# GLA stage of a FoX/GLA decoder step: weight tiles loaded two projection quarters sooner, the low part split one quarter later

## The reference, cut to what matters

```python
h = rmsnorm(x, ln_g)
z = h @ w_in                       # q, k, v, gates of both branches, merge gates
o_fox = softmax(q k^T * scale + forget sums) v      # prompt: causal; sample: over paged cache_k, cache_v
o_gla = scan over chunks of 64: att = tril((q e^b)(k e^-b)^T); o = att v + (q e^b) S; S = e^b_last S + ...
a = (o_fox * silu(fg)) @ w_up_a
b = (rmsnorm(o_gla) * silu(gg)) @ w_up_b
y = x + (sigmoid(ma) * a + sigmoid(mb) * b) @ w_out
```

## Time and profile before

| | us |
|---|---|
| median of 3 runs | 1595.02 (1590.80 to 1600.67) |
| the profiled execution | 1588.89 |
| its span, first to last instruction | 1587.2 |
| TensorE busy | 1447.4 (91%) |
| VectorE busy | 726.3 (46%) |
| ScalarE busy | 565.3 (36%) |
| GpSimd busy | 528.7 (33%) |
| mean granted TensorE clock, share of full | 0.972 |

### The profile page before, as it was taken

How to read it: one execution, slowest core, us unless ns; L and a number is a source line. 1 busy time by engine, 2 the same in 40 slices (tenths; PEclk the granted TensorE clock), 3 DMA queues, 4 the chain that set the end, 5 groups by cost and what they waited for, 6 DMA issues and landing times. The chain is left out here.

```text
span 1587.2 us, 43486 instructions
## 1 busy us (share of the span) xinstructions
PE 1447.4 (91%) x16281; PEld 1226.6 (77%) x16281; DVE 726.3 (46%) x1578; ACT 565.3 (36%) x1311; POOL 528.7 (33%) x953
## 2 busy tenths in 40 slices
PE   5999898989978897999989999889998899999998
PEld 5878777777767876788877888768876798888876
DVE  4344353543636555655546545655554223333221
ACT  6343444444532334323443334423334353111100
POOL 4444434440047135344353534454251122111000
PEclk9989999999989999999999999989999999999999
DMA  5131301222238688899997999879985764321521
GB/s 173 32 85 34 85 24 54 72 58 68 55 114 212 189 233 216 225 238 235 239 248 206 263 244 243 219 217 244 231 198 158 224 249 139 108 101 62 167 92 60
DMA packets 153411, 250.51 MB, mean 158 GB/s; under 512 B 45897, under 2 KB 58826, under 8 KB 152690
## 3 DMA queue, kind: packets, MB, share of 16 engines
q1 hardware_dynamic: 121618, 215.68, 49.8%
q0 software_dynamic: 31584, 32.04, 7.3%
HBM read 217.37 MB, written 30.22 MB: 156 GB/s over the span
## 5 line engine op out<-in xcount | busy, mean ns | idle before, releaser
L289 PE MATMUL psum<-h_hi,w_hi 128*128 128x384 f32 (+1 forms) x1344 | 491.0, 365 | 13.8 <-DVE q_fm L915 3.5
L289 PE MATMUL psum<-h_hi,w_lo 128*128 128x384 f32 (+1 forms) x1344 | 446.9, 332 | 0.0
L289 PE MATMUL psum<-h_lo,w_hi 128*128 128x384 f32 (+1 forms) x1344 | 446.4, 332 | 0.0
L1457 POOL DMA_DIRECT2D sc<-tmp_bias x512 | 278.3, 549 | 256.7 <-PE psum L1943 252.6
L289 PEld LDWEIGHTS psum<-h_hi,w_hi 128*128 128x128 f32 x1344 | 258.3, 192 | 67.1 <-issue 48.0
L289 PEld LDWEIGHTS psum<-h_lo,w_hi 128*128 128x128 f32 x1344 | 259.4, 193 | 2.7 <-issue 0.5
L289 PEld LDWEIGHTS psum<-h_hi,w_lo 128*128 128x128 f32 x1344 | 257.9, 192 | 0.0
L678 POOL DMA_DIRECT2D lfp<-in_cache_logf x256 | 124.1, 485 | 176.1 <-issue 176.1
L1671 DVE STREAM_TRANSPOSE k_page<-k_page 128x1024 f32<-128x1024 f32 x128 | 156.1, 1232 | 28.8 <-DMA k_page<-in_cache_k 27.8
L264 DVE TENSOR_TENSOR w_lo<-w_raw,w_hi 128x1024 fp32r<-128x1024 f32 x63 | 76.8, 1219 | 110.6 <-ACT w_hi L259 110.5
L259 ACT ACTIVATE w_hi<-w_raw 128x1024 fp32r<-128x1024 f32 x63 | 66.1, 1049 | 69.3 <-DMA w_raw<-in_w_tiles 37.9
(11 more groups left out here) (259 smaller groups left out, 2142.4 us busy)
## 6 DMA issues: line engine op xcount, KB each, us to landing
k_page<-in_cache_k SPq DMA_DIRECT2D x256, 256.0 KB, 3.8
v_page<-in_cache_v SPq DMA_DIRECT2D x256, 256.0 KB, 4.9
w_raw<-in_w_tiles SPq DMA_DIRECT2D x63, 512.0 KB, 5.6
g_pair<-tmp_gates SPq DMA_DIRECT2D x16, 544.0 KB, 4.6
sc<-tmp_bias POOLq DMA_DIRECT2D x512, 16.0 KB, 4.4
tmp_ogla<-gate POOLq DMA_DIRECT2D x4, 1088.0 KB, 6.8
g_pair<-tmp_ogla SPq DMA_DIRECT2D x8, 544.0 KB, 7.3
x_in<-in_x_prompt SPq DMA_DIRECT2D x8, 512.0 KB, 6.1
```

The costliest lines, as they stand in the source:

```text
L289: m = pe.matmul(out, wt[:, s, k, :], h[:, k, t0:t0 + w], start=(k == 0 and a == 0), stop=(k == KT_ - 1 and a == 2))
L1457: pool.dma_start(dst, src.unsqueeze(0).to_broadcast([TS, 2, 256])).then_inc(sc_in[j % SLOTS], 16)
```

## The change

Two conditions in `build_gla` are changed, nothing else. SP's `stream.load` moves from quarter (c = 1, part = 1) to quarter (c = 0, part = 3) of the same tile, past the steps that stand between these two in the list. VectorE's `split_lo` moves from quarter (0, 1) to quarter (0, 2). ScalarE's `split_hi` stays at (0, 1). No instruction is added or removed.

```diff
@@ build_gla, sync
             def z(n, c, part):
-                if c == 1 and part == 1:
+                if c == 0 and part == 3:
                     stream.load(sp, n)
@@ build_gla, vector
             def z(n, c, part):
-                if c == 0 and part == 1:
+                if c == 0 and part == 2:
                     stream.split_lo(dve, n)
```

## The result

The changed kernel takes 1588.05 us (median of 10 runs), the kernel before 1595.84 us in the same comparison; the ratio is 0.9948 with a 95% interval of 0.9923 to 0.9974. By that ratio it is 8.3 us less (0.52% of 1595.84), between 4 and 12; the medians lie 7.8 us apart. The profiled execution has a span of 1577.8 us against 1587.2; among the ten runs it is the fastest (1579.49 us), so the two profiles differ by a little more than the kernels do.

A forecast was written before the change was run, and what follows sets the result against it. TensorE was taken to bound the kernel, 741.1 of the stage's 810 us; 9.0 us from the low part plus 3 for the clock made 12.0, two thirds kept, 8 off 1595.0: 1587 us, range 1572 to 1604.

The forecast's parts named there:

- The total: Whole kernel: 8 us off the median of 1595.0, giving 1587 us; the GLA stage 6 to 10 us shorter.
- The low part: VectorE's split_lo, one quarter later, shortens TensorE's waits at n = 3, 6, 7, 23, 31, 32: 9.0 us.
- give-back: TensorE loses part of its gain at its next wait; two thirds of 12.0 us kept, 8 us.
- the clock: Half-clock stretches of TensorE after the waits at n = 31 and n = 7 go: 1.5 us each, 3 together.
- n = 31: TensorE's 2.38 us wait for the mask goes; the low part delays the next state by some 0.7; net 1.7 us.
- n = 7: TensorE's 3.43 us wait: transposition and gate step move into VectorE's waiting time, saving half, 1.7 us.
- n = 3: TensorE's 0.87 us wait: the low part's 1.2 us goes from ahead of the score step, saving 0.9 us.
- The load: SP's tile load sooner: ScalarE's tile waits fall from 35.9 to about 20 us; worth 0 to TensorE, bounds 0 and 16.
- its rival: More arrives: ScalarE's 16 us reach TensorE too, through the copies it makes in order; 1567 us, chance 0.08.
- SP at the low part: SP waiting for the low part before loading, at n = 1, 7, 24, 32: cost 0, without cover 11 us.
- Key pages: Loads ahead of key pages may delay VectorE's transposition: taken at 0, between a gain of 2 and a loss of 18 us.
- The rival built on it: Slower: 8 loads ahead of key pages delay VectorE and TensorE, 30 us less the 8 gained; 1617 us, chance 0.07.

The follow-up runs named there:

- Experiments 1 and 3: Against the kernel before, VectorE's low part one quarter later, load unmoved: in all tiles 0.9941; only at n = 3, 6, 7, 23, 31, 32 0.9937; only at the others 0.9969.
- experiment 2: Against the kernel before, the load alone two quarters sooner, low part unmoved: 1596.96 us, ratio 1.0019.
- experiment 5: Against the changed kernel, the load later, at quarter (2, 1), low part still at (0, 2): ratio to the kernel before 1.0149.
- experiment 8: Against the kernel before, the load two quarters sooner only at 8 tiles where it then precedes key pages: 0.9979; only at the 26 others: 1.0027.

## Why the prediction was right, point by point

*The total.* Forecast: 8 us off the median, 1587.0. Measured: 8.3 us (4 to 12), 1588.05. The stage was to be 6 to 10 us shorter and is 9.1 in the profiles. That the profiles come so close is in part luck: the 28 other tiles differ by 0.6 us only because TensorE stands 4.6 us longer in them while its matmuls take 4.1 us less, and nothing ties either to the low part.

*The low part.* This was the term that carried the sum, 9.0 us before give-back and 3 for the clock, kept at 8. Experiments 1 and 3 show it: alone it gives the whole, and at six tiles alone as well. Split as the forecast split it, the six tiles stand 6.9 us less where 9.0 were forecast, and have 2.7 us less in their matmuls where 3 were given to the clock. The clock's share fell at n = 31, as said, and at n = 23 and 32, which were not named; at n = 7 it went the other way. The waits of the earlier trace rows at n = 32, 31, 6 and 23 are gone but for 0.50 us at n = 32, and the next state of n = 31 is 0.73 us late, where 0.7 was forecast. By tile, forecast against the table above (with the clock stretch where one was named): n = 6 1.2 and 1.4; n = 23 1.3 and 1.9; n = 7 3.2 and 1.2; n = 31 3.2 and 3.0; n = 32 2.2 and 3.3; n = 3 0.9 and -1.2. The six sum to 12.0 and 9.6. At n = 7 the wait was there still, and half clock after it too, but the transposes come 1.8 us sooner, where 1.7 was forecast: that term was right and the clock's wrong.

n = 3 is where the forecast failed. The wait of 0.87 us went, and the next one took it. The score matmuls need ScalarE's last copy of the turned queries, which ends 14.9 us after the tile's start in both kernels; before and changed:

```profile
538.52 1.94 PE L1924 MATMUL psum<-k_page,q_row 128*32 128x64 f32 x64 [3.22 <-issue]
```

```profile
533.50 1.09 ACT L1506 ACTIVATE q_row<-psum 32x128 f32<-32x128 f32 x4
...
534.69 1.94 PE L1924 MATMUL psum<-k_page,q_row 128*32 128x64 f32 x64 [4.28 <-issue]
```

The profile names nothing for these two waits; that they end with the copy is read from the times (538.42 and 534.59). Behind the longer stand the clock stayed at half for longer: the projection matmuls that follow are granted 0.50 over 3.4 us in the changed kernel, and 0.72 over 2.4 us before. So a gain of 0.9 became a loss of 1.2. The tile has 20.8 to 22.7 us in the five profiles with its low part unmoved and 22.0 to 24.2 in the eight with it moved.

*The load.* Taken at 0 between -2 and +18; the load alone measured 1.0019, so +3 us with an interval of -2 to +8. The value taken stands. Of ScalarE's eight waits the first and the one at n = 18 stayed, 7.6 and 4.6 us, as argued. The third that was to stay (4.4 us, n = 28) and the 2.2 us that were to be left at n = 20 were ended by TensorE and no longer by the tile: `split_hi` also waits for the tile before to be projected, and that became the later of the two. So this wait fell to 12.2 us and not to 20, but ScalarE still stands at these two places, 3.54 and 5.59 us. Both kinds of its wait before the copy together fell from 56.5 to 44.0 us. The claim behind it, that these waits don't reach TensorE, is what experiment 2 shows, and experiment 5 that it ends. The rule that the forecast quoted from the Trainium skill (DMA: Bandwidth & Descriptors, Rules for kernel authors), to issue early and wait late, was borne out in part for ScalarE's waits (35.9 to 12.4 us with the load alone, two of eight left), and its rival, that more than 16 us would come of it, was not: the time stayed.

*SP at the low part.* Forecast: under 12 us, at no cost. Measured 9.9 us in 4 waits, at n = 1, 7, 24 and 32 as the list had it (3.4, 3.9, 1.5 and 1.1 us, where 5, 2, 2 and 2 were forecast), and the score waits behind it shrank by as much (124.5 to 113.3).

*Key pages.* The forecast named a rise of over 10 us in this wait, with TensorE's along, as a sign against it. The wait rose by 15.7, TensorE's did not. As a sign it was badly chosen: experiment 8 and the rows beside it show that it moves by more than that between kernels whose loads stand at the same places. The rival built on it, slower by way of the key pages, is out for the changed kernel; that late key pages can reach TensorE is seen at n = 3 of the low part alone, where no load was moved.

*Give-back.* The third of the 12 that I let go isn't confirmed as such. At n = 3 it is seen as forecast, the next wait takes the gain. But the six tiles keep 9.6 us in this pair, and over all profiles read their mean is 179.4 us with the low part moved and 191.3 without, 11.9 apart, about the 12.0 before give-back. In the five kernels of the table the 28 others lie between 5 us below and 4 us above the kernel before, which follows no edit. Whether the time gained is less than the 12 us because of give-back in them can't be told from this scatter.

## What to carry to other kernels

When every engine walks one list in order, look for a long side job that stands at its wait ahead of a short step on the critical chain, and move it behind that step: its own reader was 10 us away, and the job cost TensorE nothing there. A prefetch that lands late is worth moving only if the wait for it reaches the engine that sets the pace. Here 24 us less of such waits were worth nothing that can be told (1.0019, with an interval down to 0.9988), and the cover ended only somewhere before 26 of 34 tiles were late.

## What was not expected

In the changed kernel's profile TensorE stops in the middle of a group of 64 value matmuls, between two that wait for nothing the profile shows (columns of the timeline as in the earlier trace rows):

```profile
909.61 0.75 PE L1958 MATMUL psum<-v_page,p_t 128*32 128x64 f32 x36
912.70 1.07 PE L1958 MATMUL psum<-v_page,p_t 128*32 128x64 f32 x28 [2.33 <-issue]
```

Such stops of 2.3 to 2.6 us come at n = 11, 19 and 27 there, and these tiles are 3.0, 3.0 and 2.5 us longer than in the kernel before. The profile before has such stops as well, 3.07 us at n = 7 and 2.78 at n = 15; the one at n = 7 cost nothing, since TensorE would have waited there anyway. Tile n = 19 is 20 us long in some profiles and 23 to 27 in others, whatever was changed. One such stop is worth about a third of the gain of this change, which is one reason why single profiles disagree by several us and the tiles had to be compared one by one. What causes the stop is open: packets of the instruction queue were in flight at each of the three, but they come 2 to 15 us apart all through the stage.
